# The vector engine shifts half of every second tile in two RMSNorms of a Mamba, attention and expert backbone

## Chip, cores and metric

The kernel runs on 1 core of a Trainium2 chip. The metric is the time of one execution on the device in microseconds (us). Engines are called PE (TensorE; its weight loads are PEld), DVE (VectorE), ACT (ScalarE), POOL (GpSimd) and SP (SyncE, which issues nearly all DMAs).

## What is computed

The backbone has two layers over 512 tokens of width 1024: 256 context tokens and 256 latent tokens. Layer 0 is a bidirectional Mamba-2 mixer and a dense SwiGLU, layer 1 windowed attention and a top-2-of-8 expert SwiGLU. Before each of the four mixers stands the same step, an RMSNorm with its modulation; `scale` and `shift` differ for context and latent tokens:

```python
def rmsnorm(x, w):
    xf = x.astype(F32)
    y = xf * lax.rsqrt(jnp.mean(xf * xf, axis=-1, keepdims=True) + EPS)
    return (y * w.astype(F32)).astype(x.dtype)

def modulate(h, shift, scale):
    return h * (1 + scale[:, None, :]) + shift[:, None, :]
...
        hx = modulate(rmsnorm(x, norm2_w[i]), mod_x[:, 3], mod_x[:, 4])
        hc = modulate(rmsnorm(cx, norm2_w[i]), mod_c[:, 3], mod_c[:, 4])
        h = jnp.concatenate([hc, hx], axis=1)
        f = swiglu(h, ffn_w1[j], ffn_w3[j], ffn_w2[j])
```

## The kernel before

Activations lie transposed: width on the partitions, tokens along the free dimension. `xT` and `hT` are 8 tiles of 128x512 each (k = 0 to 7); columns 0 to 255 of a tile are the context tokens, columns 256 to 511 the latent tokens. Products keep float32 precision by splitting each operand in a rounded top part (type fp32r) and the rest, and adding three products (`thrice`, L663 to L665: top times top, rest times top, top times rest). The split of activations is `h_top` (ACT copies `hT`) and `h_low` (DVE subtracts). The dense weights are split in the same way: `dense_high` (ACT, L1298) and `dense_low` (DVE, L1724) handle one unit of 128x2048 each.

Each engine runs its own written-out program in order, and semaphores tie them. Two of the four norms hand their result over split and tile by tile: norm 1 (ahead of the SwiGLU's first weight unit w1) and norm 2 (ahead of the attention's first unit q0, which uses columns 256 to 511 alone). Both work like this:

1. ACT squares the tiles, PE sums them over the partitions, ACT takes the root, DVE the reciprocal (L1699), and PE spreads the result over all partitions in the bank `ps[7]` (L628).
2. DVE multiplies tile k by it: `hT = xT * ps[7]` (L1713), and counts `n_mul`.
3. ACT scales and shifts tile k in place in two ACTIVATE instructions, one for each half of 256 columns, since scale (`alpha`) and shift (`modT`) are columns that differ for context and latent tokens (L1262, `one_tile`), and counts `n_id` once a tile.
4. ACT copies the tile rounded to `h_top` (L1277, `top_tile`), and counts `n_top`.
5. DVE subtracts: `h_low = hT - h_top` (L1716), and counts `n_low`.
6. PE waits for `n_low` of tile k in the first unit that reads it (w1 or q0), and does the six matmuls of that tile.

ACT's order (`split_tiles`, L1279) is shift of tile k, then top part of tile k-1; after the third top part it splits the next weight unit once (L1298). DVE's order (`norm_split`, L1708) is the multiplication of tile k, then `h_low` of tile k-2, and behind all tiles the `dense_low` of the weight unit that follows (w3 behind w1, q1 behind q0). `h_low` of tile k-2 waits for `n_top`. Norm 0 is written apart in the program, and norm 3 has no split; both use `shifted` too.

Of the kernel before, what the change touches and what calls it, by code (L numbers as in the profile page):

```python
# [19 lines left out]
ALU = mybir.AluOpType  # L20
# [5 lines left out]
KT = D // P  # L26
NTOK = 512
NCTX = 256
NLAT = 256
EPS = 1e-6  # L30


D_INNER = 2048
# [251 lines left out]
def backbone(nc, xt_in, vecs, wdt_in, bv_in, fw_in, dense, experts_w, consts, out):  # L285
    es = ExitStack()
    with es:
# [7 lines left out]
        def sb(name, n, dt=F32):  # L295
            nonlocal top
            place_of[name] = top
            top += 4 * (n + (-n) % 8)
            assert top <= SB_BASE + 4 * SB_WORDS, (name, top)
            return at(name, place_of[name], n, dt)  # L300
# [9 lines left out]
        hT = sb("hT", KT * NTOK)[:].rearrange("p (k t) -> p k t", k=KT)  # L310
# [3 lines left out]
        modT = sb("modT", 192)[:].rearrange("p (l m r) -> p l m r", l=2, m=48)  # L314
        alpha = sb("alpha", 64)[:].rearrange("p (n k r) -> p n k r", n=4, k=8)
# [172 lines left out]
        S = {}  # L488
# [745 lines left out]
        def _(act):  # L1234
# [15 lines left out]
                r = slice(0, 64 if lat else P)  # L1250
                A(rs[r, 0:P], ps[7][r, 0:P], ACT.Sqrt, bias=eps[r], scale=1.0 / D).then_inc(S["n_rs"], 1)

            def shifted(j, l, shift, sem, lat=False):

                def one_tile(k):
                    act.wait_ge(S["alpha_done"], k // 2 + 1 if j == 0 else j + 4)
                    act.wait_ge(S["n_mul"], 8 * j + k + 1)
                    for r in range(2):
                        if lat and r == 0:
                            continue  # L1260
                        v = hT[:, k, r * 256:r * 256 + 256]
                        last = A(v, v, ACT.Identity, bias=modT[:, l, shift * 8 + k, r:r + 1],  # L1262
                                 scale=alpha[:, j, k, r:r + 1])
                    last.then_inc(S[sem], 1)
                return one_tile

            def norm_act(j, l, shift, lat=False):

                squares(j, range(KT), lat)
                root(j, lat)  # L1270
                one_tile = shifted(j, l, shift, "n_h", lat)
                for k in range(KT):
                    one_tile(k)

            def top_tile(j, k):
                act.wait_ge(S["n_id"], 8 * j + k + 1)
                A(h_top[:, k, :], hT[:, k, :], ACT.Copy).then_inc(S["n_top"], 1)  # L1277

            def split_tiles(j, l, shift, si):  # L1279

                one_tile = shifted(j, l, shift, "n_id")
                for k in range(KT + 1):
                    if k < KT:
                        one_tile(k)
                    if k:
                        top_tile(j, k - 1)
                    if k == 3:
                        dense_high(si)

            def dense_high(si):  # L1290

                n = D_AT[SPLITS[si]]
                u = D_SLOT[n]
                act.wait_ge(d_in[u], D_ARRIVED[n])
                if si >= D_HIGH:
                    act.wait_ge(S["d_used"], D_AT[SPLITS[si - D_HIGH]] + 1)
                w = dense_width(SPLITS[si])
                A(d_hi[si % D_HIGH][:, 0:w], d_raw[u][:, 0:w], ACT.Copy).then_inc(S["dhi_done"], 1)  # L1298

            def gate_high(c):  # L1300

                a, w = G_CHUNKS[c]
                if a < 4 or a >= 12:
                    act.wait_ge(S["gT_done"], a + w)
                else:
                    act.wait_ge(S["reload_in"], 32)
                if a < 8:
                    act.wait_ge(S["d_used"], D_AT[("z", 7, 0)] + 1)
                elif a == 8:
                    act.wait_ge(S["conv_step"], 128)  # L1310
                else:
                    act.wait_ge(S["m_done"], 8)
                top, _, src = gate_parts(a, w)
                A(top, src, ACT.Copy).then_inc(S["ghi_done"], 1)
# [84 lines left out]
            squares(0, range(KT))  # L1399
            root(0)  # L1400
            one_tile = shifted(0, 0, 0, "n_id")
            dense_high(0)
            for p in range(4):
# [105 lines left out]
            squares(1, (6, 7))  # L1509
            root(1)  # L1510
            split_tiles(1, 0, 3, W0 + 9)

            def hid_high(b):
# [13 lines left out]
            for j in range(4):  # L1527
# [3 lines left out]
                squares(2, (2 * j, 2 * j + 1))  # L1531
            root(2)
            split_tiles(2, 1, 0, W0 + 43)

            for i, x in enumerate((("q", 0, 0), ("q", 1, 0), ("k", 0, 0), ("q", 2, 0), ("q", 3, 0))):
# [156 lines left out]
        def _(dv):  # L1692
            TS, TT, STT = dv.tensor_scalar, dv.tensor_tensor, dv.scalar_tensor_tensor

            def norm_inverse(j, lat=False):

                dv.wait_ge(S["n_rs"], j + 1)
                r = slice(0, 64 if lat else P)
                dv.reciprocal(rs[r, 0:P], rs[r, 0:P]).then_inc(S["n_rinv"], 1)  # L1699
                dv.wait_ge(S["n_bc"], j + 1)  # L1700
# [4 lines left out]
                for k in range(KT):  # L1705
                    TT(hT[:, k, t0:t0 + nt], xT[:, k, t0:t0 + nt], ps[7][:, 0:nt], ALU.mult).then_inc(S["n_mul"], 1)

            def norm_split(j):  # L1708

                norm_inverse(j)  # L1710
                for k in range(KT + 2):
                    if k < KT:
                        TT(hT[:, k, :], xT[:, k, :], ps[7][:], ALU.mult).then_inc(S["n_mul"], 1)  # L1713
                    if k >= 2:
                        dv.wait_ge(S["n_top"], 8 * j + k - 1)
                        TT(h_low_[:, k - 2, :], hT[:, k - 2, :], h_top[:, k - 2, :].bitcast(F32), ALU.subtract)\  # L1716
                            .then_inc(S["n_low"], 1)

            def dense_low(si):

                n = D_AT[SPLITS[si]]
                u, w = D_SLOT[n], dense_width(SPLITS[si])
                dv.wait_ge(S["dhi_done"], si + 1)
                TT(d_lo[u][:, 0:w], d_raw[u][:, 0:w], d_hi[si % D_HIGH][:, 0:w].bitcast(F32), ALU.subtract)\  # L1724
                    .then_inc(S["dlo_done"], 1)
# [55 lines left out]
            dv.memset(csT, 0.0)  # L1781
            dv.memset(eps, EPS).then_inc(S["dcol_op"], 1)
            dv.memset(raw[:, :, :, 0:2], 0.0)
            dv.memset(raw[:, :, :, 258:260], 0.0).then_inc(S["dcol_op"], 1)
            dv.wait_ge(S["vecs_in"], 16)
            for q in range(2):
                r = slice(64 * q, 64 * q + 64)
# [37 lines left out]
            v, e, w, lw, dt_, a_ = (t[0:64, :] for t in dts)  # L1825
# [205 lines left out]
            def residual(k, bank, l, gate):  # L2031

                for r in range(2):
                    v = xT[:, k, r * 256:r * 256 + 256]
                    last = STT(v, ps[bank][:, r * 256:r * 256 + 256], modT[:, l, gate * 8 + k, r:r + 1], v,
                               ALU.mult, ALU.add)
                last.then_inc(S["xres"], 1)

            def out_residual(j):
                dv.wait_ge(S["d_used"], D_AT[("wout", j, 1)] + 1)  # L2040
                for t in range(2):
                    residual(2 * j + t, (0, 1, 2, 3, 4, 5, 0, 1)[2 * j + t], 0, 2)
# [7 lines left out]
            out_residual(2)  # L2050
            dense_low(W0 + 8)
            out_residual(3)
            norm_split(1)
            dense_low(W0 + 9)

            for b in range(FF_BLOCKS):
# [15 lines left out]
            for j in range(4):  # L2072
# [11 lines left out]
                dv.wait_ge(S["d_used"], D_AT[("w2", j, 2)] + 1)  # L2084
                for t in range(2):
                    residual(2 * j + t, ((4, 5), (0, 1))[j % 2][t], 0, 5)
            norm_split(2)
            dense_low(W0 + 43)

            def rope(n):  # L2090
# [93 lines left out]
            for k in range(KT):  # L2184
# [8 lines left out]
                v = xT[:, k, 256:512]  # L2193
# [9 lines left out]
            r = 0  # L2203
# [157 lines left out]
            for tt in range(2):  # L2361
# [4 lines left out]
                for hf in range(2):  # L2366
                    j = 2 * tt + hf
# [33 lines left out]
```

## Time and profile before

| | us |
|---|---|
| three runs | 2168.95, 2172.19, 2172.44 |
| median | 2172.19 |
| the profiled execution | 2173.24 |
| its span, first to last instruction | 2171.1 |
| PE busy in it | 2098.2 (97%) |
| DVE busy | 1493.2 (69%) |
| ACT busy | 1208.7 (56%) |

Some 2 us of the profiled execution lie outside its span. Norm 1 with its splits runs at 552 to 567 us of the span, norm 2 at 970 to 986 us. Start times below are counted from the span's start. Instructions of one engine overlap a little at their ends, so the start of one to the start of the next is shorter than one's duration.

### The profile page before, as it was taken

How to read it: one execution, taken by the hardware profiler on the slowest of the kernel's cores; microseconds unless marked ns; L12 is line 12 of the kernel's file. 1: busy time of each engine (PE TensorE's matmuls, PEld its weight loads, DVE VectorE, ACT ScalarE, POOL GpSimd, SP SyncE). 2: the span in 40 equal slices, each digit the busy share in tenths (PEclk: the TensorE clock that was granted, in tenths of full speed). 3: DMA queues.
4: the chain of work that ended last, by engine and by line, in shares of the span. 5: the costliest groups of instructions: out<-in, count | busy, mean ns of one | idle time of the engine just before them, and what ended most of it. 6: DMA issues, size and time to landing. Idle time of an engine off the chain costs nothing.

```text
span 2171.1 us, 26868 instructions
## 1 busy us (share of the span) xinstructions
PE 2098.2 (97%) x11254; PEld 1688.0 (78%) x11254; DVE 1493.2 (69%) x1433; ACT 1208.7 (56%) x1258; POOL 64.0 (3%) x20
## 2 busy tenths in 40 slices
PE   7999999899899999989999999999999999999997
PEld 4788888777677777868677888888888888888885
DVE  3788888853423233235659879888887988888796
ACT  4656656632422222234747776676777667676764
POOL 0111112100000000000000000000000000000000
PEclk9999999999999999999999999999999999999999
DMA  8234444422244444222237999898998989899892
GB/s 319 100 136 167 181 177 165 185 78 97 101 180 165 155 173 166 93 102 100 117 127 283 359 345 356 339 351 341 367 346 342 358 338 350 342 368 347 341 358 81
DMA packets 71777, 510.08 MB, mean 235 GB/s; under 512 B 7969, under 2 KB 8353, under 8 KB 10977
## 3 DMA queue, kind: packets, MB, share of 16 engines
q1 hardware_dynamic: 71568, 508.15, 61.7%
q8 instruction: 91, 1.49, 0.3%
q14 instruction: 38, 0.30, 0.0%
q10 hardware_dynamic: 80, 0.13, 0.0%
HBM read 504.97 MB, written 3.28 MB: 234 GB/s over the span
## 4 chain that ended last, share of the span: by engine, by line
PE 84%; DVE 9%; ACT 3%; issue 2%; DMA 2%; SPq 0%; DVEq 0%; ACTq 0%
PE ps L1113 15%; PE ps L1111 15%; PE ps L1112 14%; PE ps L663 10%; PE ps L665 10%; PE ps L664 10%; PE ps L1095 1%; DMA d_raw<-in_dense 1%; DVE area L1866 1%; PE ps L782 1%; PE ps L1142 1%; PE ps L675 1%; DVE area L1917 1%; DVE d_lo L1724 1%; PE ps L1175 1%
## 5 line engine op out<-in xcount | busy, mean ns | idle before, releaser
L2200 DVE TENSOR_TENSOR w_lo<-w_raw,w_hi 128x2048 fp32r<-128x2048 f32 x336 | 748.1, 2285 | 46.9 <-ACT w_hi L1598 46.9
L1598 ACT ACTIVATE w_hi<-w_raw 128x2048 fp32r<-128x2048 f32 x336 | 624.5, 1916 | 71.2 <-PE ps L1113 70.1
L1724 DVE TENSOR_TENSOR d_lo<-d_raw,d_hi 128x2048 fp32r<-128x2048 f32 (+1 forms) x76 | 171.8, 2260 | 298.1 <-ACT d_hi L1298 298.1
L1111 PE MATMUL ps<-w_hi,x_hi 128*128 128x512 f32 x896 | 357.2, 399 | 1.1 <-DVE x_lo L2256 1.1
L1113 PE MATMUL ps<-w_hi,x_lo 128*128 128x512 f32 x896 | 355.1, 396 | 0.0
L1112 PE MATMUL ps<-w_lo,x_hi 128*128 128x512 f32 x896 | 350.7, 391 | 0.0
L1298 ACT ACTIVATE d_hi<-d_raw 128x2048 fp32r<-128x2048 f32 (+1 forms) x76 | 143.8, 1892 | 363.6 <-DMA d_raw<-in_dense 225.7
L663 PE MATMUL ps<-h_top,d_hi 128*128 128x512 f32 (+1 forms) x816 | 327.0, 401 | 15.0 <-DVE h_low L1716 10.8
L665 PE MATMUL ps<-h_top,d_lo 128*128 128x512 f32 (+1 forms) x816 | 319.2, 391 | 0.0
L664 PE MATMUL ps<-h_low,d_hi 128*128 128x512 f32 (+1 forms) x816 | 315.0, 386 | 0.0
L663 PEld LDWEIGHTS ps<-h_top,d_hi 128*128 128x128 f32 x816 | 155.7, 191 | 58.9 <-issue 22.1
L1113 PEld LDWEIGHTS ps<-w_hi,x_lo 128*128 128x128 f32 x896 | 167.8, 187 | 41.5
L1112 PEld LDWEIGHTS ps<-w_lo,x_hi 128*128 128x128 f32 x896 | 168.5, 188 | 40.2
L1111 PEld LDWEIGHTS ps<-w_hi,x_hi 128*128 128x128 f32 x896 | 168.0, 187 | 38.6 <-DVE x_lo L2256 1.4
L665 PEld LDWEIGHTS ps<-h_top,d_lo 128*128 128x128 f32 x816 | 155.6, 191 | 34.7
L664 PEld LDWEIGHTS ps<-h_low,d_hi 128*128 128x128 f32 x816 | 156.3, 192 | 32.7
L1111 PE MATMUL ps<-w_hi,h_hi 128*128 128x512 f32 x448 | 178.5, 398 | 1.4 <-DVE h_lo L2272 1.4
L1113 PE MATMUL ps<-w_hi,h_lo 128*128 128x512 f32 x448 | 177.4, 396 | 0.0
L1112 PE MATMUL ps<-w_lo,h_hi 128*128 128x512 f32 x448 | 175.3, 391 | 0.0
L1113 PEld LDWEIGHTS ps<-w_hi,h_lo 128*128 128x128 f32 x448 | 83.9, 187 | 20.7
L1112 PEld LDWEIGHTS ps<-w_lo,h_hi 128*128 128x128 f32 x448 | 84.2, 188 | 20.0
L1111 PEld LDWEIGHTS ps<-w_hi,h_hi 128*128 128x128 f32 x448 | 84.0, 188 | 20.2 <-DVE h_lo L2272 1.7
(296 smaller groups left out, 2490.4 us busy)
## 6 DMA issues: line engine op xcount, KB each, us to landing
w_raw<-in_experts SPq DMA_DIRECT2D x336, 1024.0 KB, 4.8
d_raw<-in_dense SPq DMA_DIRECT2D x120, 1024.0 KB, 5.8
area<-acum_rows SPq DMA_DIRECT2D x16, 1024.0 KB, 7.6
d_raw<-in_dense SPq DMA_DIRECT2D x4, 768.0 KB, 4.4
xT<-in_xt SPq DMA_DIRECT2D x4, 512.0 KB, 6.7
gate_rows<-area SPq DMA_DIRECT2D x4, 512.0 KB, 6.8
hT<-gate_rows SPq DMA_DIRECT2D x2, 1024.0 KB, 6.0
cst<-in_consts SPq DMA_DIRECT2D x2, 512.0 KB, 12.9
```

The lines of the kernel that those rows point to most:

```text
L663: mm(o, w[0], v[0], start=first, stop=False)
L664: mm(o, w[0], v[1], start=False, stop=False)
L665: return mm(o, w[1], v[0], start=False, stop=last)
L675: last = mm(ps[6][c0:c0 + 32, 0:256], csT[:, k, :], d_raw[D_SLOT[n]][:, 256 * k:256 * k + 256], start=k < 4, stop=k >= 4)
L782: last = mm(o, l, r, start=n == 0, stop=n == len(steps) - 1)
L1111: mm(o, hi, w_hi[u % HIGH][:, a:a + 512], start=first, stop=False)
L1112: mm(o, hi, w_lo[u % RAW][:, a:a + 512], start=False, stop=False)
L1113: return mm(o, lo, w_hi[u % HIGH][:, a:a + 512], start=False, stop=last)
L1298: A(d_hi[si % D_HIGH][:, 0:w], d_raw[u][:, 0:w], ACT.Copy).then_inc(S["dhi_done"], 1)
L1598: A(w_hi[n % HIGH][:], w_raw[n % RAW][:], ACT.Copy).then_inc(S["whi_done"], 1)
L1724: TT(d_lo[u][:, 0:w], d_raw[u][:, 0:w], d_hi[si % D_HIGH][:, 0:w].bitcast(F32), ALU.subtract)\
L2200: TT(w_lo[n % RAW][:], w_raw[n % RAW][:], w_hi[n % HIGH][:].bitcast(F32), ALU.subtract)\
```

## The change

In norms 1 and 2, the shift of columns 256 to 511 of the odd tiles (1, 3, 5 and 7) goes from ACT to DVE, as one TENSOR_SCALAR with a multiplication and an addition. DVE does it at the end of its step k, behind the multiplication of tile k and behind `h_low` of tile k-2, and counts `n_mul` again. The other half of an odd tile and both halves of the even tiles stay on ACT. ACT's wait ahead of tile k now asks for DVE's shift too, where k is odd. The table `N_MUL` holds the counts that `n_mul` has at the start of each norm.

```diff
+N_MUL = (0, 8, 20, 32)
...
-            def shifted(j, l, shift, sem, lat=False):
+            def shifted(j, l, shift, sem, lat=False, shared=False):
...
                     act.wait_ge(S["alpha_done"], k // 2 + 1 if j == 0 else j + 4)
-                    act.wait_ge(S["n_mul"], 8 * j + k + 1)
+                    act.wait_ge(S["n_mul"], N_MUL[j] + k + 1 + ((k + 1) // 2 if shared else 0))
                     for r in range(2):
-                        if lat and r == 0:
+                        if lat and r == 0 or shared and r == 1 and k % 2:
                             continue
...
-                one_tile = shifted(j, l, shift, "n_id")
+                one_tile = shifted(j, l, shift, "n_id", shared=True)
...
-            def norm_split(j):
+            def norm_split(j, l, shift):
...
                         TT(h_low_[:, k - 2, :], hT[:, k - 2, :], h_top[:, k - 2, :].bitcast(F32), ALU.subtract)\
                             .then_inc(S["n_low"], 1)
+                    if k < KT and k % 2:
+                        dv.wait_ge(S["alpha_done"], j + 4)
+                        dv.wait_ge(S["n_mul"], N_MUL[j] + k + 1 + k // 2)
+                        v = hT[:, k, 256:512]
+                        TS(v, v, alpha[:, j, k, 1:2], modT[:, l, shift * 8 + k, 1:2], ALU.mult, ALU.add)\
+                            .then_inc(S["n_mul"], 1)
...
-            norm_split(1)
+            norm_split(1, 0, 3)
...
-            norm_split(2)
+            norm_split(2, 1, 0)
```

DVE in norm 1 before, from the first multiplication (L1713) to `h_low` (L1716) of tile 2:

```order
L1713 TENSOR_TENSOR hT<-xT,ps 128x512 [waits n_bc]
L1713 TENSOR_TENSOR hT<-xT,ps 128x512 x2
L1716 TENSOR_TENSOR h_low<-hT,h_top 128x512 [waits n_top]
L1713 TENSOR_TENSOR hT<-xT,ps 128x512
L1716 TENSOR_TENSOR h_low<-hT,h_top 128x512 [waits n_top]
L1713 TENSOR_TENSOR hT<-xT,ps 128x512
L1716 TENSOR_TENSOR h_low<-hT,h_top 128x512 [waits n_top]
```

The same stretch of DVE's program in the changed kernel, whose lines there are 1714, 1717 and, for the new shift, 1723:

```order
L1714 TENSOR_TENSOR hT<-xT,ps 128x512 [waits n_bc]
L1714 TENSOR_TENSOR hT<-xT,ps 128x512
L1723 TENSOR_SCALAR hT<-hT,alpha,modT 128x256 [waits n_mul,alpha_done]
L1714 TENSOR_TENSOR hT<-xT,ps 128x512
L1717 TENSOR_TENSOR h_low<-hT,h_top 128x512 [waits n_top]
L1714 TENSOR_TENSOR hT<-xT,ps 128x512
L1717 TENSOR_TENSOR h_low<-hT,h_top 128x512 [waits n_top]
L1723 TENSOR_SCALAR hT<-hT,alpha,modT 128x256 [waits n_mul,alpha_done]
L1714 TENSOR_TENSOR hT<-xT,ps 128x512
L1717 TENSOR_TENSOR h_low<-hT,h_top 128x512 [waits n_top]
```

The shift of tile 1 stands right behind the multiplication of that tile; the shift of tile 3 stands behind `h_low` of tile 1, those of tiles 5 and 7 behind `h_low` of tiles 3 and 5.

ACT in norm 1 before, from the shift (L1262) of tile 1 to the top part (L1277) of tile 2:

```order
L1262 ACTIVATE hT<-hT,modT,alpha 128x256 [waits n_mul,alpha_done]
L1262 ACTIVATE hT<-hT,modT,alpha 128x256
L1277 ACTIVATE h_top<-hT 128x512 [waits n_id]
L1262 ACTIVATE hT<-hT,modT,alpha 128x256 [waits n_mul,alpha_done]
L1262 ACTIVATE hT<-hT,modT,alpha 128x256
L1277 ACTIVATE h_top<-hT 128x512 [waits n_id]
L1262 ACTIVATE hT<-hT,modT,alpha 128x256 [waits n_mul,alpha_done]
L1262 ACTIVATE hT<-hT,modT,alpha 128x256
L1277 ACTIVATE h_top<-hT 128x512 [waits n_id]
```

And the same stretch of ACT's program in the changed kernel (L1263 and L1278 there):

```order
L1263 ACTIVATE hT<-hT,modT,alpha 128x256 [waits n_mul,alpha_done]
L1278 ACTIVATE h_top<-hT 128x512 [waits n_id]
L1263 ACTIVATE hT<-hT,modT,alpha 128x256 [waits n_mul,alpha_done]
L1263 ACTIVATE hT<-hT,modT,alpha 128x256
L1278 ACTIVATE h_top<-hT 128x512 [waits n_id]
L1263 ACTIVATE hT<-hT,modT,alpha 128x256 [waits n_mul,alpha_done]
L1278 ACTIVATE h_top<-hT 128x512 [waits n_id]
```

Tiles 1 and 3 have one shift on ACT in place of two, and the one that is left carries the wait for `n_mul`. The order of the pieces is otherwise the same.

## Rows read from the trace of the kernel before

**Rows 1.** The page: busy time by engine, and the chain that ended last, by engine.

```profile
PE 2098.2 (97%) x11254; PEld 1688.0 (78%) x11254; DVE 1493.2 (69%) x1433; ACT 1208.7 (56%) x1258; POOL 64.0 (3%) x20
...
PE 84%; DVE 9%; ACT 3%; issue 2%; DMA 2%; SPq 0%; DVEq 0%; ACTq 0%
```

**Rows 2.** ACT's timeline in norm 1: start, length, instructions in all, count, idle before.

```profile
552.52 2.07 ACT L1262 ACTIVATE hT<-hT,modT,alpha 128x256 f32<-128x256 f32 x4 [3.60 <-DVE hT L1713]
554.50 0.61 ACT L1277 ACTIVATE h_top<-hT 128x512 fp32r<-128x512 f32 x1
...
556.00 0.61 ACT L1277 ACTIVATE h_top<-hT 128x512 fp32r<-128x512 f32 x1
556.53 1.09 ACT L1262 ACTIVATE hT<-hT,modT,alpha 128x256 f32<-128x256 f32 x2
557.53 0.61 ACT L1277 ACTIVATE h_top<-hT 128x512 fp32r<-128x512 f32 x1
```

**Rows 3.** DVE's timeline in norm 1, the same columns.

```profile
551.74 1.88 DVE L1713 TENSOR_TENSOR hT<-xT,ps 128x512 f32<-128x512 f32 x3 [1.83 <-PE ps L628]
555.15 0.69 DVE L1716 TENSOR_TENSOR h_low<-hT,h_top 128x512 fp32r<-128x512 f32 x1 [1.53 <-ACT h_top L1277]
555.75 0.68 DVE L1713 TENSOR_TENSOR hT<-xT,ps 128x512 f32<-128x512 f32 x1
...
566.03 1.29 DVE L1716 TENSOR_TENSOR h_low<-hT,h_top 128x512 fp32r<-128x512 f32 x2 [0.81 <-ACT h_top L1277]
567.24 2.29 DVE L1724 TENSOR_TENSOR d_lo<-d_raw,d_hi 128x2048 fp32r<-128x2048 f32 x1
```

**Rows 4.** PE's timeline in norm 1: tile 0, tile 6, what follows w1, and w3.

```profile
555.99 0.77 PE L663 MATMUL ps<-h_top,d_hi 128*128 128x512 f32 x1 [4.29 <-DVE h_low L1716]
...
566.77 0.50 PE L663 MATMUL ps<-h_top,d_hi 128*128 128x512 f32 x1
...
569.76 1.07 PE L675 MATMUL ps<-d_raw,csT 128*32 128x256 f32 x16
570.76 0.50 PE L663 MATMUL ps<-h_top,d_hi 128*128 128x512 f32 x1
```

**Rows 5.** Waits of the loads in front of w1's matmuls, 546 to 572 us: total, times, longest.

```profile
PEld ps L663 <- DVE h_low L1716: 1.0, 4, 0.3
```

**Rows 6.** DVE's TENSOR_SCALAR by form: busy us, mean ns of one.

```profile
L1969 DVE TENSOR_SCALAR atk<-dtk 128x256 f32<-128x256 f32 x1 | 0.3, 282 | 0.0
L1830 DVE TENSOR_SCALAR area<-area 64x512 f32<-64x512 f32 x1 | 0.4, 419 | 0.5 <-ACT col L1419 0.5
L1850 DVE TENSOR_SCALAR area<-area,col 64x512 f32<-64x512 f32 x1 | 0.5, 479 | 0.0
L2190 DVE TENSOR_SCALAR area<-ps,col,modT 128x256 f32<-128x256 f32 x8 | 4.3, 540 | 5.3 <-PE ps L665 5.3
```

**Rows 7.** PE's timeline in norm 2: q0's tiles and the start of q1.

```profile
977.50 0.58 PE L663 MATMUL ps<-h_top,d_hi 128*128 128x256 f32 x1
977.88 0.42 PE L664 MATMUL ps<-h_low,d_hi 128*128 128x256 f32 x1
978.10 0.42 PE L665 MATMUL ps<-h_top,d_lo 128*128 128x256 f32 x1
...
980.80 0.58 PE L663 MATMUL ps<-h_top,d_hi 128*128 128x256 f32 x1 [1.65 <-DVE h_low L1716]
...
983.83 0.39 PE L663 MATMUL ps<-h_top,d_hi 128*128 128x256 f32 x1
...
985.34 0.39 PE L663 MATMUL ps<-h_top,d_hi 128*128 128x256 f32 x1 [0.53 <-DVE h_low L1716]
...
988.14 0.39 PE L663 MATMUL ps<-h_top,d_hi 128*128 128x256 f32 x1 [1.11 <-DVE d_lo L1724]
988.37 0.28 PE L664 MATMUL ps<-h_low,d_hi 128*128 128x256 f32 x1
988.48 0.28 PE L665 MATMUL ps<-h_top,d_lo 128*128 128x256 f32 x1
```

**Rows 8.** Stretches of PE: us, busy us (instructions), granted clock, DMA share, GB/s.

```profile
546.00:550.00 4.00, 1.98 (x58) 1.00 0.73 260
...
556.00:561.00 5.00, 5.00 (x13) 0.54 0.00 0
...
984.00:988.00 4.00, 2.50 (x18) 1.00 0.00 0
```

**Rows 9.** Two more stretches of PE in the third cold spell, the same columns.

```profile
1124.00:1126.00 2.00, 0.79 (x3) 0.50 1.01 426
...
1130.00:1132.00 2.00, 2.00 (x10) 0.84 1.01 426
```

## The prediction

> **What bounds the kernel.** First the page: PE is busy for 97% of the span, and the chain of work that ended last is 84% PE, 9% DVE, 3% ACT [rows 1]. Work of DVE or ACT counts only where PE stands still for it. Norms 1 and 2 are such places. In norm 1 ACT has no gap from 552.52 on: two shifts and a top part take 1.52 us a tile (556.00 to 556.53 for the top part, 556.53 to 557.53 for the two shifts, so 0.52 and 2 x 0.50) [rows 2]. DVE idles between its pieces until `h_top` comes [rows 3], and PE starts w1 after 4.29 us without work [rows 4]; later in w1 four weight loads wait again for `h_low`, up to 0.3 us each [rows 5]. So in both norms **ACT sets the pace**. At the end of norm 2, q1 waits for DVE's `dense_low`, which stands behind the last `h_low` [rows 7].
>
> **What is removed.** Four ACTIVATEs of 256 columns in each norm. ACT is the pacing engine, so each one is worth its 0.50 us of pitch [rows 2], if nothing takes its place: 4 x 0.50 = 2.0 us a norm.
>
> **What is added.** Four TENSOR_SCALARs in each norm. The trace has none of this form, so I bound it. Below: the same size from SBUF with no column operand, 282 ns. Above: the same size with two column operands, but read from PSUM, 540 ns [rows 6]. Between them: one column operand adds 479 - 419 = 60 ns [rows 6], two 120 ns, and 282 + 120 = about **0.40 us**, which I take. It is nearest to L1969, since input and output lie in SBUF as there.
>
> The Trainium skill (VectorE: DVE Perf Modes, section on the TRN2 errata) gives 58 cycles plus half the columns at 0.96 GHz for such an instruction, by an estimate 0.19 us. By that the sum below would be about 1.3 us smaller (six shifts on the path, 0.21 us less each). The row of 282 ns speaks against the figure, as that instruction has no column operand at all.
>
> **The new wait.** ACT's shift of an odd tile now waits for DVE's shift, and behind it in ACT's order stand the top part of the tile before and all that follows. For tiles 3, 5 and 7 DVE's shift stands behind `h_low` of tile k-2, which waits for the top part that ACT does right before. So there is a round trip on the path, in which ACT has nothing to do. From the start of that top part:
>
> - the top part lasts 0.61 us [rows 2];
> - DVE's `h_low` begins 0.04 us later (554.50 + 0.61 = 555.11, start 555.15) [rows 2, 3];
> - DVE's next instruction begins 0.60 us behind it (555.15 to 555.75) [rows 3];
> - the shift lasts 0.40 us;
> - ACT begins 0.10 us after DVE's end: the first multiplication began at 551.74, lasts 0.68 us and ends at 552.42, ACT starts at 552.52 [rows 2, 3].
>
> That is 1.75 us, where ACT before went on after 0.52 us. ACT idles for 1.23 us and saves 0.50 us: **+0.73 us** for each of tiles 3, 5 and 7, so +2.2 us. For tile 1 nothing stands in front of DVE's shift: its multiplication ends 0.60 + 0.68 = 1.28 us after the first one's start, the shift at 1.68, ACT could take it at 1.78 and is itself free at about 0.78 + 2 x 0.50 = 1.78 us. No wait there, and -0.50 us. The sum is **+1.7 us a norm**.
>
> Where it lands, norm 1. `h_low` of tiles 0 and 1 comes 0.5 us earlier, that of tiles 2 and 3 about 0.2 us later, 4 and 5 about 1.0, 6 and 7 about 1.7 us later. PE starts w1 0.5 us earlier, which gives nothing, as tile 6 is the last that PE waits for: its matmuls began at 566.77, with the `h_low` of tile 6 begun at 566.03 [rows 3, 4]. It begins at 568.5 then, and w1 ends 1.7 us later. Does w3 wait for its `dense_low` next? That began at 567.24 and takes 2.29 us [rows 3]; 1.7 us later it ends at 571.2, while w3 begins at 570.76 + 1.7 = 572.5 [rows 4]. It stays covered.
>
> Norm 2: q1 waited for DVE's `dense_low` and began at 988.14 [rows 7]. That is queued behind the last `h_low`, so q1 begins 1.7 us later, at 989.8. After each norm PE goes on without a gap for a long stretch, and later loads are released by PE's own progress, so I count nothing as absorbed: 2 x 1.7 = 3.5 us with the rounding.
>
> **The clock.** In norm 2 PE runs at the lower level (1.2 GHz) until 983.83, where the lengths fall from 0.58 to 0.39 us [rows 7]. What it did before: gapped work, then from 980.80 on nearly dense work for 3.0 us. In norm 1 the dense work from 555.99 ran at the lower level for 4.6 us: a granted clock of 0.54 over 556 to 561 us means 4.6 us at 0.5 [rows 4, 8]. In a third cold spell it took from 1125.2 (0.79 us busy of the stretch to 1126) to 1130.6 (0.84 over 1130 to 1132), 5.4 us [rows 9]. After the change q0's later tiles come in gapped pairs, 1.28 us of matmuls (six at 0.21 us, 977.88 to 978.10 [rows 7]) and then up to a microsecond of nothing, and the work is dense only from tile 6 on, at 985.34 + 1.7 = 987.1. With 3.0 to 5.4 us of dense work the clock rises at 990.1 to 992.5, while q1 starts at 989.8: 0.3 to 2.7 us of q1 at the lower level. A matmul of 256 columns takes 0.21 us at one level and 0.12 at the other (988.37 to 988.48) [rows 7], so 0.45 of that time is lost: 0.1 to 1.2 us. I take **0.7 us**.
>
> **The sum** is 3.5 + 0.7 = **+4.2 us**. The profiled execution took 2173.24 us, so it would come to 2177.4. It lies 1.05 us above the median of 2172.19, and on that the forecast is **2176.4 us**, 0.19% more. About 0.2% (4.3 us) is what a measurement of this kernel can tell from no change, so the forecast stands right at that line, on its near side.
>
> **The rivals.**
>
> *ACT is relieved.* If the shifts on DVE were ready whenever ACT came to them, all 8 ACTIVATEs would be gone from the path: 8 x 0.50 = -4.0 us, 2168.2 us. DVE's idle time before `h_low` [rows 3] speaks for it. Against it is the order: three of four shifts stand behind an `h_low` that waits for ACT. It decides at 0.50 us, the wait on ACT at which the saving is used up; I work out 1.23 us. The Trainium skill (ScalarE: Activation LUTs, rules for kernel authors) says to do `mul` and `add` on VectorE rather than ScalarE; by that rule the change comes out here. Chance 0.04.
>
> *Clearly slower, through the clock in w1.* PE's work in w1 becomes gapped after tile 2: tile 4 waits some 0.8 us and tile 6 again. At 546 to 550 us PE was busy for 1.98 of 4 us and the clock was lowered right after; at 984 to 988 it was busy for 2.50 of 4 and stayed up [rows 8]. In w1 it would be busy for about 2.8 of 4.2 us around tiles 3 and 4, nearer to the second. If it is lowered there, two tiles of w1 run at the lower level. Their six matmuls have 512 columns, so twice the prices above: 6 x 0.43 = 2.6 in place of 6 x 0.23 = 1.4 us each, +2.3 us on top, +6.5 us, 2178.7 us. The price decides from the first such tile on. A cold spell that lasts through more of q1 belongs here too. Chance 0.15.
>
> *The clock is not lost, or the shift is short.* If q1 starts at the higher level, +3.5 us, 2175.7; with shifts of 0.28 us, six of them 0.12 us shorter, +2.8 us. Chance 0.11.
>
> *Half is hidden.* PE waits in w1 for at most 0.3 us at a time [rows 5], so that norm 1 might cost little if PE's own pace were the limit: norm 2 alone gives +1.7 us, 2173.9. Against it: a delay of 1.7 us is far more than PE's room there. Chance 0.08.
>
> That the change doesn't reach the chip's program is excluded by the order of instructions, which has the new shifts in place.
>
> **The numbers.** The forecast, both norms longer and part of q1 cold, spans +3.6 to +4.9 us, and with the shift's upper bound (six of them 0.14 us longer) to +5.7; chance 0.62, a bit over half of it beyond 4.3 us once the upper bound is in: 0.32 slower, 0.30 same. Clock in w1: 0.15, slower. Not lost 0.11 and half hidden 0.08: same. Relief 0.04: faster. Slower 0.47, same 0.49, faster 0.04. The range from 2174.4 (+2.2) to 2178.8 (+6.6) leaves out relief, half hidden and a small part of the clock's case, and has room below for a median that falls 1 us low, as the three runs lie 3.5 us apart.
>
> **What would show it.** On ACT, an idle time of about 1.2 us in front of the shift of tiles 3, 5 and 7, ended by DVE `hT` of the new line, and none at tile 1; the new instruction at 0.40 us; PE's first matmul of w1 0.5 us sooner after the spread, and tile 6 about 1.7 us later; q1 1.7 us later with its first matmuls at the lower level. Wrong would be no idle time on ACT there, shifts far from 0.4 us, or a PE that makes up the delay before the end.

## The result and the profile after

| | before | changed |
|---|---|---|
| median of the runs timed together | 2169.95 us (12 runs) | 2176.24 us (12 runs) |
| ratio of the runs | | 1.0025, 95% interval 1.0016 to 1.0035 |
| the profiled execution, its span | 2171.1 us | 2175.0 us |
| DVE busy | 1493.2 us | 1498.1 us |
| ACT busy | 1208.7 us | 1205.9 us |

The change makes the kernel 0.25% slower, 5.4 us of 2170 (3.5 to 7.6 us by the interval). The middle of it is just past the 0.2% that the prediction called the line, while its own +4.2 us lay just short; the interval reaches to both sides of that line.

ACT's timeline in norm 1 of the changed kernel (start, length, count, idle before and what ended it), against [rows 2]:

```profile
551.24 1.72 ACT L1263 ACTIVATE hT<-hT,modT,alpha 128x256 f32<-128x256 f32 x3 [3.02 <-DVE hT L1714]
552.87 0.61 ACT L1278 ACTIVATE h_top<-hT 128x512 fp32r<-128x512 f32 x1
553.38 1.08 ACT L1263 ACTIVATE hT<-hT,modT,alpha 128x256 f32<-128x256 f32 x2
554.37 0.61 ACT L1278 ACTIVATE h_top<-hT 128x512 fp32r<-128x512 f32 x1
556.13 0.60 ACT L1263 ACTIVATE hT<-hT,modT,alpha 128x256 f32<-128x256 f32 x1 [1.15 <-DVE hT L1723]
556.63 0.61 ACT L1278 ACTIVATE h_top<-hT 128x512 fp32r<-128x512 f32 x1
```

Before, ACT had no gap here. Now it idles 1.15 us in front of its half of tile 3, and the releaser is the new shift. From the top part at 554.37 to the shift at 556.13 are 1.76 us, where 0.53 us stood before (556.00 to 556.53). Tiles 5 and 7 show the same gap; the group of the new line counts six such waits in the two norms:

```profile
L1723 DVE TENSOR_SCALAR hT<-hT,alpha,modT x8: 407/410/414, 551.9 to 986.4; 128x256 f32<-128x256 f32 x8
...
  ACT hT L1263: 6.9, 6
```

(min, median and max of one in ns; then who waited for it, us and times.) DVE's timeline in norm 1, against [rows 3], shows why the shift of tile 3 is late:

```profile
550.46 1.28 DVE L1714 TENSOR_TENSOR hT<-xT,ps 128x512 f32<-128x512 f32 x2 [1.25 <-PE ps L629]
551.85 0.41 DVE L1723 TENSOR_SCALAR hT<-hT,alpha,modT 128x256 f32<-128x256 f32 x1
...
555.01 0.69 DVE L1717 TENSOR_TENSOR h_low<-hT,h_top 128x512 fp32r<-128x512 f32 x1 [0.21 <-ACT h_top L1278]
555.62 0.41 DVE L1723 TENSOR_SCALAR hT<-hT,alpha,modT 128x256 f32<-128x256 f32 x1
...
566.63 1.29 DVE L1717 TENSOR_TENSOR h_low<-hT,h_top 128x512 fp32r<-128x512 f32 x2 [1.25 <-ACT h_top L1278]
567.84 2.29 DVE L1731 TENSOR_TENSOR d_lo<-d_raw,d_hi 128x2048 fp32r<-128x2048 f32 x1
```

The shift at 555.62 stands behind `h_low` of tile 1, which had waited for ACT's top part of 554.37. The yardstick for all that follows is the **stretch** from the first multiplication of a norm to the start of the `dense_low` behind it: 551.74 to 567.24, 15.50 us, before [rows 3], and 550.46 to 567.84, 17.38 us, now. Norm 2 has the same lengths, 15.49 and 17.38 us. DVE's timeline there, before (q1 began at 988.14 [rows 7]):

```profile
970.31 1.88 DVE L1713 TENSOR_TENSOR hT<-xT,ps 128x512 f32<-128x512 f32 x3 [1.25 <-PE ps L628]
...
985.80 2.29 DVE L1724 TENSOR_TENSOR d_lo<-d_raw,d_hi 128x2048 fp32r<-128x2048 f32 x1
```

and in the changed kernel, with PE's first matmul of q1:

```profile
971.84 1.28 DVE L1714 TENSOR_TENSOR hT<-xT,ps 128x512 f32<-128x512 f32 x2 [2.17 <-PE ps L629]
...
989.22 2.29 DVE L1731 TENSOR_TENSOR d_lo<-d_raw,d_hi 128x2048 fp32r<-128x2048 f32 x1
...
991.56 0.58 PE L664 MATMUL ps<-h_top,d_hi 128*128 128x256 f32 x1
```

So q1 begins 19.72 us after the first multiplication where it was 17.83. PE's timeline in norm 1 (tiles 0 and 6 of w1, what follows w1, w3), against [rows 4]:

```profile
554.35 0.77 PE L664 MATMUL ps<-h_top,d_hi 128*128 128x512 f32 x1 [3.93 <-DVE h_low L1717]
...
567.38 0.50 PE L664 MATMUL ps<-h_top,d_hi 128*128 128x512 f32 x1 [0.61 <-DVE h_low L1717]
...
570.36 1.07 PE L676 MATMUL ps<-d_raw,csT 128*32 128x256 f32 x16
571.36 0.50 PE L664 MATMUL ps<-h_top,d_hi 128*128 128x512 f32 x1
```

Counted from the first multiplication, w1 ends after 19.90 us (570.36 - 550.46) where it was 18.02 (569.76 - 551.74), and w3 follows 1.00 us later as before: it stays covered.

**Where the 3.9 us between the two profiled spans lie.** Between landmarks of the two timelines: from the start to norm 1's first multiplication -1.28 us; from there to the end of w1 +1.88; to norm 2's first multiplication +0.93, all of it in norm 2's spread, whose matmuls ran at the lower clock level this time; from there to q1 +1.89; q1 itself 6.26 us in place of 5.80, +0.46; all the rest +0.02. The sum is +3.90 us. The change owns +1.88, +1.89 and +0.46, so 4.2 us; the -1.28 lies ahead of it.

### The profile page after: what moved, and what is told of

It reads as the page before. It is cut to its first block, busy times and chain, and to the rows that moved or that the text cites. A ratio compares the mean times of both kernels' runs of the same rounds, so it can differ in the third digit from the quotient of the medians.

```text
span 2175.0 us, 26876 instructions
## 1 busy us (share of the span) xinstructions
PE 2097.6 (96%) x11254; PEld 1687.6 (78%) x11254; DVE 1498.1 (69%) x1441; ACT 1205.9 (55%) x1250; POOL 61.7 (3%) x20
## 3 DMA queue, kind: packets, MB, share of 16 engines
q8 instruction: 91, 1.49, 0.3%
## 4 chain that ended last, share of the span: by engine, by line
PE 82%; DVE 10%; ACT 4%; issue 2%; DMA 2%; SPq 0%; DVEq 0%; ACTq 0%
PE ps L1114 15%; PE ps L1112 14%; PE ps L1113 14%; PE ps L664 10%; PE ps L666 10%; PE ps L665 9%; DVE area L1873 2%; DMA d_raw<-in_dense 1%; PE ps L1096 1%; PE ps L1143 1%; PE ps L783 1%; PE ps L676 1%; DVE d_lo L1731 1%; DVE area L1924 1%; PE ps L1176 1%
## 5 line engine op out<-in xcount | busy, mean ns | idle before, releaser
L664 PE MATMUL ps<-h_top,d_hi 128*128 128x512 f32 (+1 forms) x816 | 328.1, 402 | 17.6 <-DVE h_low L1717 13.6
```

Source lines behind the costliest of these rows:

```text
L664: mm(o, w[0], v[0], start=first, stop=False)
```

## The experiments

All times are ratios to the kernel before, timed together. The stretches and lengths are from one profile each. The first four versions below the change were timed in one set, against the same 30 runs of the kernel before, and the last three in another, against the same 29; the last section comes back to what that does to the ratios.

| kernel | stretch in norm 1, norm 2 (us) | first multiplication to end of w1, to q1 | q1 | ratio (95%) |
|---|---|---|---|---|
| before | 15.50, 15.49 | 18.0, 17.8 | 5.80 | 1 |
| the change | 17.38, 17.38 | 19.9, 19.7 | 6.26 | 1.0025 (1.0016 to 1.0035) |
| shift ahead of h_low | 14.90, 14.89 | 17.6, 17.2 | 5.79 | 0.9989 (0.9980 to 0.9999) |
| three tiles ahead | 13.62, 13.62 | 17.4, 16.0 | 5.79 | 0.9982 (0.9971 to 0.9992) |
| wait without saving | 19.33, 19.36 | 21.9, 21.7 | 6.58 | 1.0030 (1.0018 to 1.0042) |
| tile 1 alone | 15.14, 15.14 | 17.7, 17.5 | 5.91 | 0.9990 (0.9980 to 1.0000) |
| norm 1 alone | 17.38, 15.49 | 19.9, 17.8 | 5.80 | 1.0011 (1.0000 to 1.0023) |
| norm 2 alone | 15.49, 17.37 | 18.0, 19.7 | 5.80 | 1.0012 (1.0002 to 1.0023) |
| the change, PE filled | 17.38, 17.38 | 19.9, 19.7 | 5.79 | 1.0020 (1.0011 to 1.0030) |

The theory is the **round trip**: the shift on DVE comes late because it stands behind an `h_low` that waits for ACT. Its rival is **DVE's added work**: four instructions of 0.41 us in DVE's chain cost their time wherever they stand.

### The shift ahead of h_low

In `norm_split`, the `h_low` of tile k-2 goes behind the shift:

```diff
                     if k < KT:
                         TT(hT[:, k, :], xT[:, k, :], ps[7][:], ALU.mult).then_inc(S["n_mul"], 1)
-                    if k >= 2:
-                        dv.wait_ge(S["n_top"], 8 * j + k - 1)
-                        TT(h_low_[:, k - 2, :], hT[:, k - 2, :], h_top[:, k - 2, :].bitcast(F32), ALU.subtract)\
-                            .then_inc(S["n_low"], 1)
                     if k < KT and k % 2:
...
                         TS(v, v, alpha[:, j, k, 1:2], modT[:, l, shift * 8 + k, 1:2], ALU.mult, ALU.add)\
                             .then_inc(S["n_mul"], 1)
+                    if k >= 2:
+                        dv.wait_ge(S["n_top"], 8 * j + k - 1)
+                        TT(h_low_[:, k - 2, :], hT[:, k - 2, :], h_top[:, k - 2, :].bitcast(F32), ALU.subtract)\
+                            .then_inc(S["n_low"], 1)
```

> The yardstick is the stretch from the first multiplication of a norm to the start of the dense_low behind it: 15.5 us before, 17.4 us with the change, in both norms. Round-trip theory (the shift comes late only because it stands behind h_low of tile k-2, which waits for ACT): with the shift in front of that h_low, ACT's wait for tiles 5 and 7 goes and 0.5 us is left at tile 3; DVE's own work becomes the limit in part, since its two-tile cycle is then about 2.9 us. The stretch takes 14.9 us in both norms, 2.5 us less than with the change, and the kernel comes out at or a little below the time before (-1 to 0 us against it). Rival (the added DVE work, 4 x 0.41 us in DVE's chain, costs its time wherever it stands): the stretch stays near 17.1 to 17.4 us, the kernel some 4 us above the time before.

The stretches are 14.90 and 14.89 us, the forecast of the round trip. The same instructions, moved by one place, give 2.5 us a norm back. ACT's timeline in norm 1 shows what is left, at tiles 3 and 6:

```profile
553.71 0.60 ACT L1263 ACTIVATE hT<-hT,modT,alpha 128x256 f32<-128x256 f32 x1 [0.44 <-DVE hT L1719]
...
558.05 0.59 ACT L1263 ACTIVATE hT<-hT,modT,alpha 128x256 f32<-128x256 f32 x1
...
559.56 1.10 ACT L1263 ACTIVATE hT<-hT,modT,alpha 128x256 f32<-128x256 f32 x2 [0.40 <-DVE hT L1714]
```

At tile 3 the shift is still 0.44 us late; tile 5 (558.05) finds its shift ready. At tile 6 ACT waits 0.40 us for a multiplication. DVE's timeline in front of that start at 559.56:

```profile
558.18 0.69 DVE L1723 TENSOR_TENSOR h_low<-hT,h_top 128x512 fp32r<-128x512 f32 x1 [1.49 <-ACT h_top L1278]
558.79 0.68 DVE L1714 TENSOR_TENSOR hT<-xT,ps 128x512 f32<-128x512 f32 x1
```

The multiplication of tile 6 stands behind `h_low` of tile 3, and DVE idled 1.49 us for ACT's top part of that tile before it could begin. So this wait isn't a lack of DVE time alone; it is a round trip once more, now through a multiplication, and the next experiment takes it away.

By the table, w1 ends 0.4 and q1 begins 0.6 us sooner after the first multiplication than before, 1.0 us together. The ratio says 2.4 us (0.2 to 4.3), more than the 0 to 1 us expected, with an interval that holds both.

### Multiplications three tiles ahead

DVE's order becomes multiplication of tile k+3, `h_low` of tile k, shift of tile k+3 where that is odd:

```diff
+                times(0)
+                times(1)
+                shift_half(1)
+                times(2)
+                for k in range(KT):
+                    if k + 3 < KT:
+                        times(k + 3)
+                    dv.wait_ge(S["n_top"], 8 * j + k + 1)
+                    TT(h_low_[:, k, :], hT[:, k, :], h_top[:, k, :].bitcast(F32), ALU.subtract)\
+                        .then_inc(S["n_low"], 1)
+                    if k + 3 < KT and k % 2 == 0:
+                        shift_half(k + 3)
```

> DVE multiplies three tiles ahead of h_low, and shifts tile k+3 right behind h_low of tile k, so that the shift has a whole tile of time before ACT wants it. Round-trip theory: no wait of ACT on a shift after tile 1, all four saved ACTIVATEs count, and the stretch takes 13.5 us (15.5 - 4 x 0.5) in both norms. w1 ends only 0.5 to 1.2 us sooner than before, since there PE itself becomes the limit in part; q1 begins 2.0 us sooner but may run longer at the lower clock level. The kernel: 1.5 to 3 us below the time before. Rival (the added DVE work costs its time wherever it stands): 17.1 us or more.

13.62 us in both norms. The shift of tile 3 runs at 555.71 and ends at 556.12, before ACT comes to its half at 556.48. DVE's and then ACT's timeline in norm 1:

```profile
555.10 0.69 DVE L1730 TENSOR_TENSOR h_low<-hT,h_top 128x512 fp32r<-128x512 f32 x1
555.71 0.41 DVE L1718 TENSOR_SCALAR hT<-hT,alpha,modT 128x256 f32<-128x256 f32 x1
```

```profile
556.48 0.59 ACT L1263 ACTIVATE hT<-hT,modT,alpha 128x256 f32<-128x256 f32 x1
556.97 0.61 ACT L1278 ACTIVATE h_top<-hT 128x512 fp32r<-128x512 f32 x1
```

DVE does exactly the work that the changed kernel gives it, and the stretch is 3.8 us shorter a norm: the rival falls. Of the 1.9 us won against the kernel before, norm 2 passes on all (17.8 to 16.0 us), norm 1 only 0.6 us (18.0 to 17.4), since PE has become the limit in w1: after tile 0 it has no gap there. That is 2.5 us by the profiles. The ratio of 0.9982 is the lowest of the study, 3.9 us below the kernel before (1.7 to 6.3 us); 1.5 to 3 were expected. Its interval overlaps those of the shift ahead of `h_low` and of tile 1 alone, so only the stretches tell these three apart. The new order with all shifts left on ACT wasn't run. That it would give nothing by itself is argued from ACT, which had no gap in the kernel before [rows 2].

### The wait without the saving

DVE's instruction writes to a scratch tile (`sil`), so its work is left without effect, and ACT waits for it but shifts all halves:

```diff
-                        if lat and r == 0 or shared and r == 1 and k % 2:
+                        if lat and r == 0:
...
-                        TS(v, v, alpha[:, j, k, 1:2], modT[:, l, shift * 8 + k, 1:2], ALU.mult, ALU.add)\
+                        TS(sil[0][:, 0:256], v, alpha[:, j, k, 1:2], modT[:, l, shift * 8 + k, 1:2], ALU.mult, ALU.add)\
```

> The wait without the saving: DVE's instruction writes to a scratch tile that nobody reads, at the same place and with the same counts, and ACT waits for it but does all sixteen shifts itself. Round-trip theory: ACT idles 1.15 us by the profile's count at tiles 3, 5 and 7 and about 0.1 us at tile 1, with no saving: 15.5 + 3 x 1.24 + 0.1 = 19.3 us, 3.8 us more than before in each norm, the kernel +7.6 us and what the clock takes. Rival (DVE's work is what costs): as with the change, 17.4 us, the kernel +4 us.

19.33 and 19.36 us, as the round trip asks. In ACT's timeline the same gap is now followed by two ACTIVATEs:

```profile
553.15 0.61 ACT L1278 ACTIVATE h_top<-hT 128x512 fp32r<-128x512 f32 x1
554.90 1.09 ACT L1263 ACTIVATE hT<-hT,modT,alpha 128x256 f32<-128x256 f32 x2 [1.15 <-DVE sil L1723]
```

So the wait alone costs 3.83 us a norm, and the four saved ACTIVATEs give 1.95 us back. The kernel's time rose by 6.5 us (3.9 to 9.1) where 7.6 and more were expected and the lengths in the table give 8.5; the interval holds all of these.

### Tile 1 alone

```diff
-N_MUL = (0, 8, 20, 32)
+N_MUL = (0, 8, 17, 26)
...
-                        if lat and r == 0 or shared and r == 1 and k % 2:
+                        if lat and r == 0 or shared and r == 1 and k == 1:
...
-                    if k < KT and k % 2:
+                    if k == 1:
```

> The change for tile 1 alone, where nothing stands in front of DVE's shift. Round-trip theory: no round trip, one ACTIVATE saved less about 0.1 us of wait, the stretch 15.15 us in both norms (-0.35), the kernel -0.7 us, which is too little to tell in its time. Rival (DVE's work costs): +0.4 us a norm, 15.9 us.

15.14 us in both norms: the one shift without a round trip is a gain of 0.35 us. In the changed kernel, then, tile 1 gives 0.35 us and tiles 3, 5 and 7 take 2.23, 0.74 us each. The interval of the time ends at 1.0000, so it doesn't tell this from no change, as expected.

### One norm at a time

The shift on DVE and its counts in norm 1 or in norm 2 alone (`shared=j == 1`, or 2, and the same condition on DVE).

> The change in norm 1 alone. Round-trip theory: norm 1's stretch 17.4 us, norm 2's 15.5 us, the kernel +1.9 us; q1 takes 5.8 us, at the higher clock level from its start, as in the kernel before. If the delay of norm 1 were hidden by what follows, the kernel would show +0.

> The change in norm 2 alone. Round-trip theory with a share of the clock: norm 1's stretch 15.5 us, norm 2's 17.4 us, and q1 partly at the lower level, 0.3 to 3.5 us of it, so that q1 takes 5.9 to 7.4 us; the kernel +2.0 to +3.5 us. Without a share of the clock: q1 5.8 us, the kernel +1.9 us.

Each norm shows its own 17.4 us and leaves the other at 15.5, and each alone makes the kernel slower by 0.11% or 0.12%, 2.4 and 2.6 us. The delay of norm 1 isn't hidden: the time says so weakly, as its interval begins at 1.0000, but in the profile the way from the end of w1 to norm 2's first multiplication is 401.48 us, no shorter than the 400.55 us before. One expectation failed: with norm 2 alone q1 took 5.80 us, at the higher clock level from its start. PE's stretches there (us, busy us and instructions, granted clock, DMA):

```profile
980.00:984.00 4.00, 3.39 (x15) 0.50 0.00 0
984.00:988.00 4.00, 2.36 (x16) 0.86 0.07 8
988.00:994.00 6.00, 5.91 (x49) 1.00 0.46 172
```

The level rose between 984 and 988 us, in q0's last tiles, before q1 began at 988.09. Norm 2 has the changed kernel's program here, and in the profiles of that kernel q1 takes 6.24 to 6.41 us. So the clock takes its share in some executions and not in others; what decides it isn't shown.

### PE filled in norm 2

The changed kernel, with matmuls added to norm 2 whose result nobody reads: five behind the spread, and 4, 10, 4 and 4 behind tiles 1, 2, 3 and 5 of q0.

```diff
             norm_spread(2)
+            for _ in range(5):
+                mm(ps[6][:, 0:256], ident, cst[:, 0:256], start=True, stop=True)
...
+                    if i == 0:
+                        for _ in range((0, 4, 10, 4, 0, 4, 0, 0)[k]):
+                            mm(ps[6][:, 0:256], dense_tile(n, k, 0)[0], h_top[:, k, 256:512], start=True, stop=True)
```

> The change in both norms, and in norm 2 PE is given matmuls whose result nobody reads, between the spread and tile 0 and in the gaps behind tiles 1, 2, 3 and 5. If the clock takes a share because PE's work in q0 is gapped: the level is high from the middle of q0 on and through q1, q1 takes 5.8 us, and the kernel is 0.5 to 1.5 us faster than with the change (+3.8 to +4.5 us against the time before). If the clock has no share: the same as with the change. The two stretches on DVE stay at 17.4 us, or norm 2's is longer where the filling delays a tile.

PE's stretches, first in the changed kernel:

```profile
984.00:988.00 4.00, 3.38 (x14) 0.50 0.00 0
988.00:992.00 4.00, 3.38 (x15) 0.50 0.00 0
992.00:994.00 2.00, 2.00 (x16) 0.85 0.56 143
```

and with the filling:

```profile
984.00:988.00 4.00, 2.68 (x20) 1.00 0.00 0
988.00:992.00 4.00, 2.87 (x24) 1.00 0.52 168
992.00:994.00 2.00, 2.00 (x19) 1.00 0.48 197
```

The stretch of norm 2 is the same 17.38 us, the level stays up, and q1 takes 5.79 us. That is 0.47 us less than in the profile of the change, the price of the lower level in q1. The ratio of 1.0020 isn't told apart from the change's 1.0025.

### Both kernels again

> The kernel before once more, for a second profile: q1 at the higher clock level from its start and 5.8 us long, both stretches 15.5 us. If the spread of its times comes from the phase of the clock's rises and falls, the time of the spread matmuls after norm 2's reciprocal (1.2 us at one level, 2.1 at the other) and of the first tiles differs from the first profile, and the sum of those differences is the difference in time.

> The changed kernel once more, beside the kernel before on one chip. By the parts seen so far (two stretches of 17.4 in place of 15.5 us, q1 some 0.5 us longer) it is 4.3 us, 0.2%, slower. If something outside the two norms and q1 were part of the cost, the ratio would stay at 0.25% or more and the pieces between them would differ in the profile by more than the 0.9 us that the spread takes at the lower clock level.

> A third profile of the changed kernel. Both stretches 17.4 us. If the clock's share in q1 depends on when the level rises, q1 takes another length than 6.26 us, between 5.8 and 7.4; without a share of the clock all profiles agree.

> A fourth profile of the changed kernel, for the same question: both stretches 17.4 us, q1 between 5.8 and 7.4 us and another length than in the others if the clock has a share.

> The kernel before, timed against itself, and a third profile of it. If the intervals of this study are sound, the ratio is 1.000 and its interval holds 1; both stretches 15.5 us, q1 5.8 us. If a kernel can differ from itself by 0.1% in such a comparison, the 0.38% of the run before this one is the 4.3 us of the parts and such an offset, and nothing else has to be found. If the ratio is within 0.05% of 1, some 2 to 4 us of the changed kernel's time in that run lie in places that the profiles don't show.

The first and the last are the kernel before, the three between them the changed one. The spans of the two more profiles before were 2172.0 and 2166.5 us, those of the changed kernel 2174.7, 2177.7 and 2177.1. In all of them the stretches are 15.5 before and 17.4 after, and q1 takes 5.78 and 5.80 us before and 6.24, 6.32 and 6.41 us after. With the first profiles, q1's mean is 5.79 against 6.31 us: +0.52 us for the clock. So the part of the change is 1.88 + 1.89 + 0.52 = **4.3 us**, 0.20%.

The timed ratio of the change was 1.0038 (1.0024 to 1.0052) in this set, and that of the kernel before against itself 1.0005 (0.9995 to 1.0014). The 4.3 us lie inside the interval of the first comparison and under that of the second, whose low end is 5.2 us. The kernel before against itself moved by 0.05% only. So one or more microseconds may be real and outside the two norms and q1. Against that stand the other sets. The lengths in the table give -1.0, -2.5, +8.5 and -0.5 us for the first four versions below the change, and their ratios say -2.4, -3.9, +6.5 and -2.2 us: all four lie 1.4 to 2.0 us lower than their parts. The three of the next set lie 0.5 to 0.7 us higher. An offset of one to two microseconds that is common to a set shows with other kernels too, in both directions. The excess is 1.1 us in the change's first comparison and 3.9 us here, the latter above every offset seen; how much of it belongs to the change isn't shown. By the means of the three and four profiles the spans differ by 6.3 us: 4.3 us as above, 0.7 ahead of norm 1 where the kernels are alike, 0.4 between w1 and norm 2's first multiplication, where the spread runs at either clock level (400.55 to 401.48 us), and 0.9 behind q1 (1175.3 to 1177.4 us). Whether the later start of everything behind norm 1 makes the lower level more frequent there, or these are chance, stays open.

## Why the prediction was right

- **What bounds.** Right: ACT paces both norms, and the delay behind the last `h_low` reached PE at full length (1.88 us at the end of w1, 1.89 us at q1).
- **What is removed.** 0.50 us of ACT for each shift. The wait-only kernel minus the change gives 1.95 and 1.98 us a norm for four.
- **What is added.** 0.40 us was taken from the row of 282 ns and 60 ns for each column operand; measured 407 to 414 ns. The 0.19 us worked out from the Trainium skill (VectorE: DVE Perf Modes, section on the TRN2 errata) is less than half of it; that section itself says that its row gives too little.
- **The new wait.** 1.75 us from top part to shift was forecast, 1.76 us measured, and +0.73 us a tile became +0.74.
- **Tile 1.** The one term of the norms that was off: -0.50 us was forecast, -0.35 measured. DVE's shift began 0.11 us after the end of the multiplication that it waits for (550.46 + 1.28 = 551.74, start 551.85), and the prediction let it begin at once, so ACT did wait a little. With that a norm costs 1.88 in place of 1.7 us. It also moved the first `h_low` and PE's start in w1: 0.36 us sooner after the first multiplication (3.89 us in place of 4.25), not 0.5.
- **Where it lands.** Right for w1, for w3 (which stayed covered) and for q1.
- **The clock.** 0.7 us taken, 0.1 to 1.2 as bounds; +0.52 us on average of four profiles, and nothing in the kernel with norm 2 alone. The way there was not quite the forecast one: the level was to stay low through q0, and it rose for tile 2 and fell again (last section). q1 did start at the lower level, at 991.56, and its matmuls are short (0.28 us) from 992.72 on. In w1 the level wasn't lowered again in any of the four profiles, though PE had gaps of 0.6 us there, so the clearly slower rival did not come true.
- **The rival of relief.** It needed a wait on ACT under 0.50 us and met one of 1.2. The rule of the Trainium skill (ScalarE: Activation LUTs, rules for kernel authors), that a multiplication and an addition belong on VectorE, paid here once the order let it: with the multiplications three tiles ahead, the same four shifts on DVE made each norm's stretch 1.88 us shorter than before.
- **The total.** +4.2 us was forecast, the parts give 4.3, the comparison 5.4 (3.5 to 7.6). The closeness of 4.2 to 4.3 is in part luck. The norms were put 0.4 us too low (3 x 0.73 - 0.50 = 1.69 us each, 3.4 for both, against 3.8 measured), the prediction's own rounding from 3.4 to 3.5 gave 0.1 us back, and the clock was put 0.2 us too high. That the median came out at 2176.24 us beside a forecast of 2176.4 has help from the base: over 12 runs the kernel before had a median of 2169.95, not 2172.19 us.

## What to carry to other kernels

When work moves from the pacing engine to another one, look at what stands in front of it in the other's order: an instruction that itself waits for the pacing engine turns the help into a round trip, and here that cost 3.8 us where the help was worth 2. The cure was order alone: run the independent producer (the multiplications) some tiles ahead, so that the moved piece is done before it is wanted (for tile 3, 0.36 us before: 556.12 against 556.48). And put a wait on one engine's own earlier result into the sum; it is small, but with what came along it took 0.15 of the 0.50 us that tile 1 could give.

## What was not expected of the hardware

A DVE instruction that waits for the DVE instruction right in front of it began 0.11 us after that one's end, while without such a wait DVE's instructions overlap: 555.01 to 555.62 is 0.61 us for an instruction of 0.69.

The granted clock moved up and down within q0 of the changed kernel. PE's timeline there, with idle time before:

```profile
979.41 0.39 PE L664 MATMUL ps<-h_top,d_hi 128*128 128x256 f32 x1 [0.61 <-DVE h_low L1717]
979.64 0.28 PE L665 MATMUL ps<-h_low,d_hi 128*128 128x256 f32 x1
...
982.71 0.58 PE L664 MATMUL ps<-h_top,d_hi 128*128 128x256 f32 x1 [2.32 <-DVE h_low L1717]
```

Tile 2 ran at the higher level (0.39 us), then PE was idle for 2.32 us while ACT split the weight unit, and tile 3 ran at the lower level again (0.58 us). All four profiles of this kernel show it. Before, the gap at this place was 1.65 us [rows 7]. It had no price in q0, whose tiles wait for `h_low` in any case.
